# Expert weights fetched as two transfers of 1 MB, with each buffer given back in two halves

## The reference

```python
def expert_block(args):
    xb, e = args
    hb = jax.nn.silu(xb @ w1[e]) * (xb @ w3[e])
    return hb @ w2[e]
```

## Time and profile before

| | us |
|---|---|
| median of 3 runs | 1469.64 (1467.89 to 1470.36) |
| the profiled execution, its time | 1469.37 |
| its span, first to last instruction | 1467.6 |
| PE busy in the span | 1396.2 (95%) |
| DMA queue of SP, share of 16 engines' span | 59.1% |

### The profile page before, as it was taken

The page is one execution under the profiler, slowest core; times in us unless marked ns, Lnnn a source line. Parts: engine busy times, 40 slices in busy tenths (PEclk is TensorE's granted clock), DMA queues, the critical chain, the costliest instruction groups (busy, mean ns, idle before and its releaser), DMA issues.

```text
span 1467.6 us, 25889 instructions
## 1 busy us (share of the span) xinstructions
PE 1396.2 (95%) x11102; PEld 1142.9 (78%) x11102; DVE 703.1 (48%) x1084; ACT 544.7 (37%) x852; POOL 20.5 (1%) x15
## 2 busy tenths in 40 slices
PE   7999998999999999999999979989999988999997
PEld 5899997879766665665666548879999976899996
DVE  6675894546621111111111056866655658665564
ACT  3455764145211111111111144655433447643342
POOL 0000002200000000000000000000000000000000
PEclk9999998999999999999999989999999999999999
DMA  9434432015779999999999992235454621345420
GB/s 392 177 152 172 173 122 110 3 58 234 311 330 422 425 426 426 424 426 426 424 426 425 425 412 77 87 139 206 177 196 170 231 101 71 142 186 202 173 86 29
DMA packets 31473, 351.98 MB, mean 240 GB/s; under 512 B 3088, under 2 KB 3344, under 8 KB 4880
## 3 DMA queue, kind: packets, MB, share of 16 engines
q1 hardware_dynamic: 31232, 349.49, 59.1%
q10 hardware_dynamic: 144, 1.05, 0.2%
HBM read 349.48 MB, written 1.05 MB: 239 GB/s over the span
## 4 chain that ended last, share of the span: by engine, by line
PE 81%; DVE 9%; ACT 4%; DMA 3%; issue 2%; DVEq 0%; ACTq 0%
PE psum L433 79%; DMA ring<-in_w 3%; DVE slot_lo L1780 2%; ACT pages L1196 1%; PE psum L523 1%; ACT mix_hi L1220 1%; DVE pages L1960 1%; PE psum L821 1%; DVE pages L2392 0%; DVE tiny L1728 0%; DVE pages L2297 0%; DVE pages L2330 0%; ACT w_hi L1220 0%; ACT gu_hi L1547 0%; DVE pages L1811 0%
## 5 line engine op out<-in xcount | busy, mean ns | idle before, releaser
L433 PE MATMUL psum<-pages 64*64 64x64 f32 (+11 forms) x3280 | 315.3, 312 | 10.2 <-ACT pages L1196 3.5
L433 PEld LDWEIGHTS psum<-pages 128*64 128x64 f32 (+4 forms) x3280 | 225.1, 153 | 86.6 <-issue 46.3
L433 PE MATMUL psum<-ring,pages 128*64 128x256 f32 (+1 forms) x1556 | 210.2, 423 | 4.2 <-DMA ring<-in_w 4.2
L433 PE MATMUL psum<-x_hi,gu_hi 128*128 128x256 f32 x704 | 199.7, 284 | 0.1
L433 PE MATMUL psum<-x_lo,gu_hi 128*128 128x256 f32 x704 | 199.2, 283 | 0.0
L433 PE MATMUL psum<-x_hi,gu_lo 128*128 128x256 f32 x704 | 199.2, 283 | 0.0
L433 PEld LDWEIGHTS psum<-ring,pages 128*64 128x64 f32 x1556 | 111.1, 137 | 89.0 <-issue 40.5
L1780 DVE TENSOR_TENSOR slot_lo<-ring,mix_hi 128x2048 fp32r<-128x2048 f32 x44 | 101.7, 2314 | 78.9 <-ACT mix_hi L1220 78.8
L433 PEld LDWEIGHTS psum<-x_hi,gu_hi 128*128 128x128 f32 x704 | 134.9, 192 | 2.2 <-DVE x_lo L1767 0.5
L433 PEld LDWEIGHTS psum<-x_lo,gu_hi 128*128 128x128 f32 x704 | 134.9, 192 | 1.6
L433 PEld LDWEIGHTS psum<-x_hi,gu_lo 128*128 128x128 f32 x704 | 134.9, 192 | 0.0
(11 more groups left out here) (227 smaller groups left out, 2198.1 us busy)
## 6 DMA issues: line engine op xcount, KB each, us to landing
ring<-in_w SPq DMA_DIRECT2D x58, 2048.0 KB, 25.7
pages<-in_w SPq DMA_DIRECT2D x38, 2048.0 KB, 26.0
ring<-in_ffn SPq DMA_DIRECT2D x44, 1536.0 KB, 6.2
ring<-in_w_in SPq DMA_DIRECT2D x16, 2048.0 KB, 8.5
ring<-in_e_in SPq DMA_DIRECT2D x3, 2048.0 KB, 39.2
ring<-in_w_pa SPq DMA_DIRECT2D x2, 2048.0 KB, 7.8
ring<-in_w_pb SPq DMA_DIRECT2D x2, 2048.0 KB, 7.9
ring<-in_w_o SPq DMA_DIRECT2D x2, 2048.0 KB, 7.5
```

What stands on the lines that cost most here:

```text
L433: return pe.matmul(o, lhsT, rhs, start=start, stop=stop, skip_group_check=True)
```

## The change

A load becomes two DMAs of 1 MB (`half_load`), each 128 rows of 8 KB: half h is columns h x 2048 to (h + 1) x 2048 of each partition. The first half counts on the semaphore of the buffer as before, the second on a new `second<b>_landed`. PE waits for the first half ahead of the product and for the second in the middle of it, at k = 4 of 8 or f = 2 of 4; the matmul ahead of that wait also counts up a new `half_read`. SP now waits for `half_read` and issues the first half of weight u + 10, then waits as before for the end of the product and issues the second half. `REUSED` lets the new names share old semaphores whose use is over, with their count as an offset: `half_read` is `vb_ready`, `second0_landed` is `x0_landed`, and so on; the rows of the instruction order show these old names.

```diff
@@ -122,6 +122,12 @@
     }
 
 
+REUSED = {f"second{n}_landed": old for n, old in enumerate(
+    (("x0_landed", 16), ("x1_landed", 16), ("start_landed", 32), ("ln_in_landed", 16), ("gm_rows_landed", 32),
+     ("mixer_landed", 48), ("wab_split", 1), ("wab_high", 1), ("gate_masked", 1), ("g_ready", 1)))}
+REUSED["half_read"] = ("vb_ready", 1)
+
+
 def stream_items():
 
     items = []
@@ -153,6 +159,8 @@
 
             if name.endswith("_tokens") and name[:-7] in NORMS:
                 return "norm_tokens", 4 * NORMS.index(name[:-7])
+            if name in REUSED:
+                return REUSED[name]
             owner, _, kind = name.partition("_")
             if owner in SECTIONS and kind in ("probs", "pT", "max", "exp", "o_ready"):
                 before = sum(list(SECTIONS.values())[:list(SECTIONS).index(owner)]) // 2
@@ -805,11 +813,18 @@
 
             act = page(10)[:, 1536:2048].rearrange("p (r s) -> p r s", r=2)
 
-            def expert_h(r, w, half):
+            def await_second(v):
+
+                pe.wait_ge(*V(f"second{v % BUFFERS}_landed", 16 * (v // BUFFERS + 1)))
+
+            def expert_h(r, w, half, v=None):
 
                 each = KD // len(w)
                 w = [piece_.rearrange("p (k c) -> p k c", k=each) for piece_ in w]
                 for k in range(KD):
+                    if v is not None and k == KD // 2:
+                        last.then_inc(S("half_read"), 1)
+                        await_second(v)
                     for g in range(2):
                         last = mm(psum[g * CAP:(g + 1) * CAP, r, half * T:(half + 1) * T], xe[:, k, r * CAP:(r + 1) * CAP],
                                   w[k // each][:, k % each, g * T:(g + 1) * T], k == 0, k == KD - 1)
@@ -821,11 +836,14 @@
                     last = pe.transpose(psum[:, 2 + r, c * P:(c + 1) * P], act[:, r, c * P:(c + 1) * P], ident)
                 return last
 
-            def expert_y(r, w2):
+            def expert_y(r, w2, v=None):
 
                 each = FE // P // len(w2)
                 w = [piece_.rearrange("p (f c) -> p f c", c=D) for piece_ in w2]
                 for f in range(FE // P):
+                    if v is not None and f == FE // P // 2:
+                        last.then_inc(S("half_read"), 1)
+                        await_second(v)
                     for g in range(2):
                         a = (f % 2) * P + (f // 2) * CAP
                         last = mm(psum[g * CAP:(g + 1) * CAP, 2 + r, :], actT[:, r, a:a + CAP],
@@ -861,8 +879,9 @@
                 pe.wait_ge(*V("xe_ready", 2 * j + 2))
                 for r in range(2):
                     pe.wait_ge(free[r], j + base[r])
-                    expert_h(r, landed_weights(6 * j + 2 * r), 0).then_inc(S("w1_read"), 1)
-                    expert_h(r, landed_weights(6 * j + 2 * r + 1), 1).then_inc(full[r], 1)
+                    v = 6 * j + 2 * r
+                    expert_h(r, landed_weights(v), 0, v).then_inc(S("w1_read"), 1)
+                    expert_h(r, landed_weights(v + 1), 1, v + 1).then_inc(full[r], 1)
                 for r in range(2):
                     pe.wait_ge(free[2 + r], 2 * j + base[2 + r])
                     scatter(r).then_inc(S("scattered"), 1)
@@ -874,7 +893,7 @@
                             pe.wait_ge(*V("picks_ready", j + 2))
                         gather(r).then_inc(S("gathered"), 1)
                     pe.wait_ge(free[2 + r], 2 * j + base[2 + r] + 1)
-                    expert_y(r, landed_weights(6 * j + 4 + r)).then_inc(full[2 + r], 1)
+                    expert_y(r, landed_weights(6 * j + 4 + r), 6 * j + 4 + r).then_inc(full[2 + r], 1)
 
             for j in range(PAIRS):
                 expert_pair(j, j == PAIRS - 1)
@@ -2574,20 +2593,29 @@
             sp.dma_start(page(12), io["ln1"][0:1, :].partition_broadcast(P)).then_inc(S("router_landed"), 16)
             if phases >= 2:
                 first_of = lambda i: io[LOADS[i % 6]][2 * (i // 6) + LOAD_OF[i % 6]]
-                halves_of = lambda src: src.rearrange("p (n c) -> p n c", c=PAGE)
+
+                def half_load(b, src, h):
+
+                    s = BUFFER_SLOTS[b]
+                    dst = spare[b][:, h, :] if s is None else ring_slot(s)[:, h * PAGE:(h + 1) * PAGE]
+                    sems = S(f"second{b}_landed") if h else spare_landed[b] if s is None else landed[s]
+                    sp.dma_start(dst, src[:, h * PAGE:(h + 1) * PAGE]).then_inc(sems, 16)
+
                 spare_free = {1: V("h_split", 8), 4: (full[place["w_pb3"][0]], place["w_pb3"][1]),
                               8: (full[place["w_o3"][0]], place["w_o3"][1]), 9: V("ln1_tokens", 4)}
                 for i, s in enumerate(BUFFER_SLOTS):
                     if s is None:
                         sp.wait_ge(*spare_free[i])
-                        sp.dma_start(spare[i], halves_of(first_of(i))).then_inc(spare_landed[i], 16)
+                        for h in range(2):
+                            half_load(i, first_of(i), h)
                         continue
                     if s < MIXER_SLOTS:
                         sp.wait_ge(*released[max(m for m in range(moe_first) if slot_no(m) == s)])
                     else:
                         b_, n_ = place["w_o3" if s == MIXER_SLOTS else "gate_b_1"]
                         sp.wait_ge(full[b_], n_)
-                    sp.dma_start(ring_slot(s), first_of(i)).then_inc(landed[s], 16)
+                    for h in range(2):
+                        half_load(i, first_of(i), h)
                 base = place["moe_base"]
 
                 def consumed(it, u):
@@ -2600,24 +2628,25 @@
                     else:
                         sp.wait_ge(full[x - 2], it * (2 * ROUND) + (2 * (u // 6) + base[x - 2] + 2))
 
-                def load_next(it, u):
+                def load_next(it, u, h):
 
                     b, v = u % BUFFERS, u + BUFFERS
                     expert = it * (2 * ROUND) + (2 * (v // 6) + LOAD_OF[v % 6])
                     src = io[LOADS[v % 6]][bass.ds(expert, 1)].rearrange("e p c -> p (e c)")
-                    if b in spare:
-                        sp.dma_start(spare[b], halves_of(src)).then_inc(spare_landed[b], 16)
+                    if h == 0:
+                        sp.wait_ge(*V("half_read", it * (6 * ROUND) + (u + 1)))
                     else:
-                        sp.dma_start(ring_slot(BUFFER_SLOTS[b]), src).then_inc(landed[BUFFER_SLOTS[b]], 16)
+                        consumed(it, u)
+                    half_load(b, src, h)
 
                 rounds = (3 * EXPERTS - BUFFERS) // (6 * ROUND)
                 with sp.Fori(0, rounds) as it:
                     for u in range(6 * ROUND):
-                        consumed(it, u)
-                        load_next(it, u)
+                        for h in range(2):
+                            load_next(it, u, h)
                 for u in range(3 * EXPERTS - BUFFERS - 6 * ROUND * rounds):
-                    consumed(rounds, u)
-                    load_next(rounds, u)
+                    for h in range(2):
+                        load_next(rounds, u, h)
                 early = moe_end
                 if phases >= 3:
                     load(early, *items[early])
```

## The result

| | before | changed |
|---|---|---|
| median, us (18 executions of each) | 1469.03 | 1472.80 |
| lowest to highest | 1467.71 to 1473.43 | 1467.79 to 1476.48 |
| ratio | | 1.0020 (95%: 1.0011 to 1.0028) |
| span of the profiled execution | 1467.6 | 1472.3 |

The change costs 0.2%, with an interval of 0.11 to 0.28%. (The medians alone stand further apart, 3.8 us or 0.26%; the means 3.1 us.) 1470.5 was forecast, within 1466.2 to 1475.0.

The account below looks back on a forecast made before the run. The expert stage was taken as bound by its string of weight loads, with PE nearly as busy; -1.7 (restart) + 4.3 (rows) - 1.7 (last product) = +0.9 us gave 1470.5 us on the median, range 1466.2 to 1475.0.

Parts of the forecast that it names:

- the fourth case: Rival: early half waits, refills and tail keep their times, only dearer 8 KB rows stay; +4.3 us, 1473.9; chance 0.12.
- Part 1: Restart of the load string: weight 10's first half issued mid-product, second following without a gap; gain 1.7 us, once.
- Part 2: Loads 10 to 95: rows shrink from 16 to 8 KB on 61 loads, 0.07 us each; loss 4.3 us.
- rows are free: Rival: 8 KB rows cost nothing, the landing difference has another source; -3.4 us, 1466.2; chance 0.12.
- Part 3: Load queue: twice as many transfers cost 0 us; SP blocks earlier, queue holds some 25 us of work.
- the rival (0.13): Rival: a seam between transfers costs DMA time, deciding from 0.025 us each; at 0.05, 1474.8; chance 0.13.
- Part 4: PE's products: 96 more waits and increments cost 0 us where the data is already there.
- Part 5: Last expert product: its first half is done before weight 95's second half lands; gain 1.7 us.
- The sum: At the scatter after the last expert product: -1.7 + 4.3 - 1.7 = +0.9 us.
- the late split of `in_e_lora`: Behind the scatter: load lands 2.6 us later, ACT's table load is pushed to 862.5; no cost, but no room.

Follow-up runs that it names:

- the square: Four kernels with all loads in halves: refill's first half issued early or late, second wait inside or ahead of the product; stages from 440.96 to 444.11 us.
- e2_both: Changed kernel, but both halves issued after the whole product and PE waiting for both ahead of it; 1475.45 us, 1.0037 against the kernel before.
- e4_late: Changed kernel, but both halves of a refill issued after the whole product, second wait still inside it; 1472.48 us, 1.0025 against the kernel before.
- e5_early: Changed kernel with its early refill, but PE waits for both halves ahead of the product; 1471.75 us, 1.0015 against the kernel before.
- e6_rows: Kernel before, one transfer a load, but weights padded in device memory so all rows are 8 KB; 1476.91 us, 1.0046.
- e7_tail: Kernel before with only weights 86 to 95 in halves, issued together, second wait inside the product; 1469.34 us, 0.9999.
- e10_tail2: The kernel of e7_tail measured again, unchanged; 1469.68 us, 0.9998 against the kernel before.
- e3_seam: As e2_both, but each load halved by partitions, 64 each, keeping the earlier row sizes; 1879.24 us, 1.2808 against the kernel before.
- e8_before: Kernel before, unchanged, profiled a second time in one execution; stage 439.64 us, first product at 415.57 us.
- e9_ends: The kernel of e7_tail with weights 10 and 40 also in halves, first half issued mid-product; 1468.94 us, 0.9993 against the kernel before.
- e12_ends2: The kernel of e9_ends measured again, unchanged; 1469.32 us, 0.9996 against the kernel before.

## Why the prediction came out as it did

The time lay in the range, 2.3 us above the forecast, and the ratio, 0.20%, just at the bound of what was said to be told from no change. Only part of that is the reckoning's merit. The terms that it prices come out at +1.3 to +1.5 us in the stage, against +0.9 forecast; the rest of the measured difference, as much again or more, lies outside the stage, where the sum has no term, and was caught by the width of the range. By its number alone 1472.8 lies nearer to the fourth case, "the halves don't do what they say" (1473.9), than to the forecast (1470.5); it is the square that rules that case out, since both gains are there. By the steps:

**Part 1, earlier restart, forecast -1.7: right in size at the end of the string, wrong in how.** The issue came 1.70 us earlier (2.17 against 3.87), and the square prices it at -1.3 to -1.7. But the step said that the second half is ready without a gap, and there was one. Windows of 1 us of the changed kernel, 424 to 428:

```profile
424.00:425.00 1.00, 1.00 (x12) 0.68 (x10) 0.00 (x0) 0.00 (x0) 0.00 (x0) 1.00 1.02 426
425.00:426.00 1.00, 1.00 (x14) 0.64 (x12) 0.00 (x0) 0.00 (x0) 0.00 (x0) 1.00 1.25 393
426.00:427.00 1.00, 1.00 (x12) 0.70 (x10) 0.00 (x0) 0.29 (x1) 0.00 (x0) 1.00 0.73 205
427.00:428.00 1.00, 1.00 (x14) 0.66 (x10) 0.42 (x1) 0.09 (x1) 0.00 (x0) 1.00 0.98 401
```

The first half lands 4.9 us after its issue (in line with 2.4 + 2.5), the second 3.9 us behind it where 2.5 was meant: throughput falls to 205 GB/s for a microsecond. In the six profiles with an early first half the second follows 3.0 to 3.9 us behind it; where both are issued together, late (e2_both, e4_late), it is the 2.5. Weight 10 as a whole lands at 10.5 to 11.0 in the changed kernel against 11.2 before. By weight 11 the kernels with all refills early (changed, e5_early: 15.2 to 15.9) lead those with halves and late refills (e2_both, e4_late: 16.6 and 16.8) by 0.7 to 1.5 us, and by weight 93 by 1.2 to 1.8. How the change gets back what it lost in that gap was not isolated.

**Part 2, rows of 8 KB, forecast +4.3: right.** This was the disputed term, read from three landings and two windows. The price of a load, 0.07, is what the medians of the steps give (4.90 and 4.97). e2_both and e6_rows put it at +4.5 and +4.8 in the stage, e4_late, which has the inner waits as well, at +3.1. By landings over 85 loads the cost is 3.2 to 4.2. The windows' 425 and 421 GB/s, means over all loads, say 4.93 and 4.98 us a load, 4.0 us over 86 of them: the two agree. (The single late landings, over 0.4 us above the median step, add up to 6.6 and 6.7 us in the kernel before and to 3.3 to 5.6 in the kernels with 8 KB rows throughout, which is why the whole string shows less than 85 steps of 0.07. Why they are fewer is open.) The rival "rows are free" (0.12) is ruled out.

**Part 3, the seams, forecast 0: right.** e2_both against e6_rows: 0.4 us over 85 seams, and with the 0.6 by which the string of the kernel before repeats at most 1.0, 0.012 us each, against the 0.025 from which the rival (0.13) would have decided. SP's issues block already at 570 us (before: 732), and the binding half at the end landed 27.00 us after its issue began, 24.9 after SP had handed it over; 25 was said.

**Part 4, waits inside a product, forecast 0: right.** Where the data is there, the weight loads of two products with three waits between them run as one piece, 6.83 us as in the earlier trace rows (timeline of PEld in the changed kernel):

```profile
426.19 6.83 PEld L441 LDWEIGHTS psum<-ring,pages 128*64 128x64 f32 x64
```

**Part 5, the last product, forecast -1.7: the size right (-1.4 to -1.8 by the square, -1.2 and -1.5 by e7_tail and e10_tail2), the place wrong.** The step had weight 95 as the load that binds, from a profile in which it did, by less than 0.3 us. In the second profile of the kernel before, and in every other kernel here, weight 93 binds: in the changed kernel its second half landed at 847.45, and from there PE, ACT and PE again need 12.96 us to the scatter, where a whole wait makes it 14.70. The prediction said that weights 86 to 93 gain the same, and that nothing earlier holds the last product up. The first is so, and is why the amount held; the second is not.

**The sum.** +0.9 was forecast at the scatter; the stage says +1.3 to +1.5 (440.96, 441.11 and 440.97 against 439.64). The landing of weight 95 is as forecast: +2.6 was the sum of parts 1 and 2, and it lands at 438.49, 438.29 and 438.04 from the start against 435.92 and 435.34, which is +2.1 to +2.6 against 435.92, the profile that the prediction read. The missed half microsecond lies in weight 93, which lands at 428.00 to 428.15 against 424.71 and 424.94 and sets the stage. That is as much as the terms of the square spread, so it can't be put down to one of parts 1 and 2. Behind the scatter nothing was lost to the late split of `in_e_lora`: ACT's split moved to 862.26 and the table load to 863.98, as worked out, and from the second half of the scatter to the next stage's first matmul the changed kernel takes 12.4 us (862.06 to 874.47), against 12.6 and 12.4 in the two profiles before (858.84 to 871.49, 856.86 to 869.28).

**What is left over: from +1.4 in the stage to +2.8 in the time.** The means are 2.8 us apart over the ten measurements used below. In the profiles, the part ahead of the stage took 419.45, 418.65 and 419.12 in the changed kernel and 417.56 and 415.57 in the one before, although PE, ACT and DVE do the same there; the part behind the scatter took 611.3 to 612.0 against 610.4 and 611.0. The windows show what goes with the first. Two stretches of the changed kernel, PE fully busy at a granted clock of 0.57:

```profile
371.00:375.00 4.00, 4.00 (x12) 3.16 (x11) 3.06 (x4) 0.73 (x1) 0.00 (x0) 0.57 1.01 426
405.00:409.00 4.00, 4.00 (x11) 2.12 (x11) 2.55 (x20) 0.21 (x1) 2.31 (x3) 0.57 1.01 422
```

(In the kernel before both places show 1.00.) At 0.57 most of each stretch runs at the lower of the two levels, 1.2 GHz. Summed over all that comes before the stage, PE's clock stood low for 17.0 us in the two executions that start at 415.6, for 20.4 in those that start at 416.7 to 417.6, for 23.8 in those from 417.7 to 419.5, and for 27.3 in e2_both, which starts at 420.26. So the start is later where the clock stood low for longer, whatever the kernel, though starts with the same 23.8 us still spread by 1.7.

To see whether this carries the remainder, the 196 executions of ten of the measurements (91 of the kernel before; without the first measurement, e3_seam and e8_before) were fitted by one term for the kernel and one for the mean granted clock: 0.93 us (standard error 0.05) for each 0.001 of clock. This is a correlation; no run sets the clock. At the same clock the changed kernel is 2.0 us slower than before (plus or minus 0.5, two standard errors, as in the brackets of the table), where the plain means differ by 2.8; its clock was 0.9822 on the mean against 0.9830. The others come out with the sign of their stages and within 1.5 us of them:

| | stage against before | time against before at equal clock |
|---|---|---|
| changed | +1.4 | +2.0 (0.5) |
| e4_late | +3.1 | +2.5 (0.7) |
| e5_early | +3.2 | +2.5 (0.7) |
| e2_both | +4.5 | +6.0 (0.8) |
| e6_rows | +4.8 | +5.4 (1.0) |
| e7_tail, e10_tail2 | -1.4 | -1.1 (0.5) |
| e9_ends, e12_ends2 | -0.8 | -1.0 (0.5) |

So of the +2.8, 1.4 is the stage, 0.8 goes with a lower clock, and 0.6, a little more than two standard errors of the fit, stays open. Whether the change itself lowers the clock (the ten first loads, which move ahead of the stage, come in halves too) or the executions fell so by chance was not settled: e7_tail, which has almost nothing of the change, had a mean clock of 0.9821 too, and e5_early, whose loads all come in halves, 0.9836.

## What to carry to other kernels

Giving a buffer back in halves brings at most half a step, once where the string of transfers restarts and once where it ends, however many loads lie between; what the finer form costs per load is paid for every load. Here 1.3 to 1.8 for each end stood against some 4.5. So split only the loads at the end, where a wait inside the last products is worth having (1.2 and 1.5 us of the stage here, too little to be told in the time), and leave the long middle in the largest rows. The early issue of the one first refill brought nothing here, and why is open. And before a tail is priced from the last transfer in the chain, see how far behind it the next path lies: here it was less than 0.3 us.

## What the runs showed of the hardware that was not expected

- **A transfer over 64 of the 128 partitions runs at half the throughput**, 219 GB/s against 421, with the DMA share at 1.01 (e3_seam: 338 packets of the queue and 4.39 MB in 20 us). A busy share of 1 is thus no evidence of full throughput. The Trainium skill's page "DMA: Bandwidth & Descriptors", section "Rules for kernel authors", advises against two transfers to disjoint halves of the partitions; the runs agree with the advice, at a ratio of 1.28. Sharing the engines one after the other does not explain it: the two transfers of e2_both do that too and move 421 GB/s.
- **A second transfer of 1 MB that is issued 1.7 us behind a cold one lands 3.0 to 3.9 us behind it** (six profiles), in place of the 2.5 of two that are issued together.
- **A cold load of 2 MB in 256 rows of 8 KB landed 8.9 us after its issue** (e6_rows, one profile), one in 128 rows of 16 KB after 7.3 to 7.7 (the earlier trace rows and three more profiles). It isn't the rows alone: the same rows as two transfers issued together (e2_both, e4_late) are there after 7.3 and 7.5.
- **SP's queue took fewer bytes when rows were smaller**: at the end of the stage a load of 2 MB lands 37.8 us after SP has handed it over in the kernel before (46.07 less the 8.24 that its issue took), a half in the changed kernel 24.9 us after (27.00 less 2.1), a load in e6_rows 28.9. By throughput that is 7.7 loads, ten halves and 5.8 loads. Once it is full each issue blocks, which cost no throughput here.
